# A transformer block in FP32 on TensorE: 32 further tokens of the first expert stage as rows of their own, dot products shared out anew, identity matmuls at the start

## What is computed

```
q = xt @ wq; sub = einsum(q, subkeys)            # scores of 2 x 128 keys, 8 heads
s_top, i_top = top_k(sub, 16)                    # per head and half
cand = s_top[0][:, None] + s_top[1][None, :]
sc, ci = top_k(cand, 16)
eid  = i1 * 128 + i2                             # 128 experts of a token
gate = softmax(sc)
h    = gelu(einsum('cd,ced->ce', x, u[eid]))     # u: 16384 x 1024
out  = einsum('ce,ced->cd', gate * h, v[eid])    # v: 16384 x 1024
h    = layer_norm(ALPHA * h + out)
```

## Time and profile before

| | us |
|---|---|
| median of 3 runs | 1701.08 |
| lowest and highest | 1700.94, 1702.02 |
| profiled execution: its own time | 1701.76 |
| profiled execution: its span | 1700.0 |

### The profile page before, as it was taken

The page is one execution under the profiler, slowest core; times in us unless marked ns, Lnnn a source line. Parts: engine busy times, 40 slices in busy tenths (PEclk is TensorE's granted clock), DMA queues, the critical chain, the costliest instruction groups (busy, mean ns, idle before and its releaser), DMA issues.

```text
span 1700.0 us, 24431 instructions
## 1 busy us (share of the span) xinstructions
PE 1671.8 (98%) x8981; PEld 1477.7 (87%) x8981; DVE 1219.6 (72%) x2490; ACT 778.9 (46%) x1318; POOL 815.4 (48%) x493
## 2 busy tenths in 40 slices
PE   7999999999999999999999999999999999999997
PEld 6777777788889999999999999999888888888886
DVE  3588995512173985989888888434988888888886
ACT  4555544522334444773676477434333333333332
POOL 6232232444551667776866777785523233322312
PEclk9999999999999999999999999999999999999999
DMA  5121122233431566997899789998999999999952
GB/s 203 64 75 50 50 75 75 87 121 116 134 112 38 177 216 197 372 380 253 287 383 371 226 318 374 369 375 291 398 401 349 373 388 349 381 378 353 382 198 87
DMA packets 126502, 417.63 MB, mean 246 GB/s; under 512 B 12976, under 2 KB 32432, under 8 KB 124848
## 3 DMA queue, kind: packets, MB, share of 16 engines
q1 hardware_dynamic: 70320, 232.81, 39.2%
q0 software_dynamic: 36864, 134.23, 21.0%
q10 hardware_dynamic: 19200, 49.03, 7.3%
HBM read 364.91 MB, written 50.86 MB: 245 GB/s over the span
## 4 chain that ended last, share of the span: by engine, by line
PE 92%; DVE 3%; DMA 2%; POOL 1%; ACT 1%; issue 1%; SPq 0%; another core or an unknown queue 0%; ACTq 0%; DVEq 0%; POOLq 0%
PE ps L1364 18%; PE ps L1365 17%; PE ps L1366 17%; PE ps L1602 10%; PE ps L1601 10%; PE ps L1604 10%; PE ps L1712 5%; PE ps L1476 1%; DMA raw<-w_units 1%; PE ps L1428 1%; POOL w_lo L458 1%; PE ps L1459 1%; DMA gelu_d<-gelu_t 1%; PE ps L1405 0%; PE ps L1425 0%
## 5 line engine op out<-in xcount | busy, mean ns | idle before, releaser
L1364 PE MATMUL ps<-tok_hi,w_hi 128*128 128x384 f32 (+1 forms) x1480 | 529.8, 358 | 5.6 <-issue 4.3
L559 ACT ACTIVATE w_hi<-raw 128x1024 fp32r<-128x1024 f32 x330 | 348.9, 1058 | 394.0 <-PE ps L1604 292.3
L1366 PE MATMUL ps<-tok_hi,w_lo 128*128 128x384 f32 (+1 forms) x1480 | 520.5, 352 | 0.0
L1365 PE MATMUL ps<-tok_lo,w_hi 128*128 128x384 f32 (+1 forms) x1480 | 520.5, 352 | 0.0
L502 POOL TENSOR_TENSOR w_lo<-raw,w_hi 128x1024 fp32r<-128x1024 f32 x128 | 318.5, 2491 | 165.6 <-ACT w_hi L559 165.1
L458 POOL TENSOR_TENSOR w_lo<-raw,w_hi 128x1024 fp32r<-128x1024 f32 x76 | 183.3, 2415 | 320.9 <-ACT w_hi L559 320.7
L1364 PEld LDWEIGHTS ps<-tok_hi,w_hi 128*128 128x128 f32 x1480 | 278.2, 188 | 37.2 <-issue 14.5
L519 POOL DMA_INDIRECT v_got<-v_rows,eid x128 | 152.4, 1191 | 301.7 <-DVE own L1148 284.8
L1601 PE MATMUL ps<-w_hi,gh_hi 128*128 128x512 f32 x760 | 295.7, 389 | 0.0
L1602 PE MATMUL ps<-w_lo,gh_hi 128*128 128x512 f32 x760 | 295.7, 389 | 0.0
L1366 PEld LDWEIGHTS ps<-tok_hi,w_lo 128*128 128x128 f32 x1480 | 278.1, 188 | 18.6
(11 more groups left out here) (240 smaller groups left out, 1941.4 us busy)
## 6 DMA issues: line engine op xcount, KB each, us to landing
raw<-u_units SPq DMA_DIRECT2D x128, 512.0 KB
raw<-v_rows SPq DMA_DIRECT2D x128, 512.0 KB
raw<-w_units SPq DMA_DIRECT2D x78, 512.0 KB
gate_d<-stage ACTq DMA_DIRECT2D x12, 2048.0 KB
gelu_d<-gelu_t ACTq DMA_DIRECT2D x120, 192.0 KB
gelu_in<-gelu_d SPq DMA_DIRECT2D x30, 768.0 KB, 7.7
gate_in<-gate_d SPq DMA_DIRECT2D x28, 768.0 KB
gate_in<-gate_d SPq DMA_DIRECT2D x2, 1536.0 KB
```

The costliest lines, as they stand in the source:

```text
L559: act.activation(hi_of(n), raw[:, n % RAW, :], ACT.Copy).then_inc(hi_done, 1)
L1364: pe.matmul(out_, l_hi, r_hi, start=start, stop=False)
L1365: pe.matmul(out_, l_hi, r_lo, start=False, stop=False)
L1366: return pe.matmul(out_, l_lo, r_hi, start=False, stop=stop)
```

## The change

The dense part of the `u` stage takes 352 columns instead of 384. The first 32 tokens of the second tile ("near") get their Gelu values from gathered rows: 32 more gathers and dot products, four groups of 32 columns beside each other, which fill 128 partitions. Their experts are spread over the partitions by four small transfers on ACT's queue (`spread_near_eid`), their `x` rows likewise (`spread_near_x`), and their results go back by four more (`finish_near`). Their gates are still built densely, but last of all quads and already multiplied with the Gelu values; so PE turns picks a fourth time (`turn_picks(4)`), ahead of quad 88, and `gelu_in` holds ones in their columns. The `v` stage keeps its 384 columns.

Around this the table is a new one: 14 first units; 19 units for each route; 13, 17 and 21 units of marks, with 24, 32 and 40 quads; 6 units behind (`TAIL` is 122). The 160 dot products are shared out as 14, 16 and 16 in the routes, at six places of each instead of three; 24, 32 and 38 in the marks; 6 behind; and 14 in the first units of `v`, where the sums with rows of `v` now begin at unit 16 and are due by unit 120 (before: 2 and 116). DVE marks two quads with one pair of instructions. POOL issues gathers in the marks up to `DOTS_BY[k - 2]` plus five. SP issues the first loads of the gates behind the loads of all units of `u`. At the start, PE runs 16 matmuls of the identity with itself (as soon as POOL has made it), and unit 1 runs its products with high weights first.

```diff
-FIRST_UNITS, ROUTE_UNITS, MARK_UNITS = 16, 14, 16
-TAIL = FIRST_UNITS + 3 * (ROUTE_UNITS + MARK_UNITS)
-ROUTE_DOTS, MARK_DOTS = (3, 6, 6), 30
+FIRST_UNITS, ROUTE_UNITS, MARK_UNITS = 14, 19, (13, 17, 21)
+TAIL = FIRST_UNITS + 3 * ROUTE_UNITS + sum(MARK_UNITS)
+ROUTE_DOTS, MARK_DOTS, TAIL_DOTS, LATE_DOTS = (14, 16, 16), (24, 32, 38), 6, 14
+NEAR_FROM, NEAR_END = 58, 58 + NEAR
...
-FMA_START, FMA_END = 2, P - 12
+FMA_START, FMA_END = LATE_DOTS + 2, P - 8
...
             for j in range(P):
                 load_unit(U_EXP + j, u_units[j])
-                if j == P - 8:
-                    sp.wait_ge(gate_read, N_QUAD)
-                    for s in range(2):
-                        sp.wait_ge(stage_out[s], 16 * (NB // 2))
-                    load_gates(0, 0)
-                if j == P - 4:
-                    load_gates(0, 1)
+            sp.wait_ge(gate_read, N_QUAD)
+            for s in range(2):
+                sp.wait_ge(stage_out[s], 16 * (NB // 2))
+            load_gates(0, 0)
             for j in range(P):
                 load_unit(U_VAL + j, v_rows[:, (j - KEPT) % P, :])
+                if j == 1:
+                    load_gates(0, 1)
...
-                rows_to(dots_by(k - 1) + U_SLOTS if k >= FIRST_UNITS + ROUTE_UNITS else 3)
+                if k < FIRST_UNITS + ROUTE_UNITS:
+                    rows_to(min(DOTS_BY[k - 1] + 3, ROUTE_DOTS[0]))
+                else:
+                    rows_to(DOTS_BY[k - 2] + U_SLOTS)
...
+            def finish_near():
+
+                act.wait_ge(dot_done, NEAR_END)
+                act.activation(near_dot[:], near_dot[:], ACT.Gelu).then_inc(near_gelu, 1)
+                act.wait_ge(near_gelu, 1)
+                for g in range(NEAR_GROUPS):
+                    part = slice(NEAR * g, NEAR * g + NEAR)
+                    act.dma_start(near_h[0:NEAR, part], near_dot[part, :]).then_inc(near_h_in, 16)
...
             def mark(q):
...
                 if q >= 4:
-                    dve.wait_ge(gate_full, q - 3)
+                    dve.wait_ge(gate_full, q - 2)
...
-                dve.tensor_tensor(left[:, s, :, :], numbers, first, ALU.is_equal)
-                dve.tensor_tensor(match[:, s, :, :], numbers, second, ALU.is_equal).then_inc(match_set, 1)
+                two = slice(q % 4, q % 4 + 2)
+                dve.tensor_tensor(left[:, two, :, :].rearrange("p s t k -> p (s t) k"), numbers, first, ALU.is_equal)
+                dve.tensor_tensor(match[:, two, :, :].rearrange("p s t k -> p (s t) k"), numbers, second, ALU.is_equal)\
+                    .then_inc(match_set, 1)
...
-                tokens = slice(P, S) if n >= U_EXP else slice(0, S)
-                to = ps[:, bank, 0:DT] if n >= U_EXP else ps[:, bank, :]
+                tokens = slice(P + NEAR, S) if n >= U_EXP else slice(0, S)
+                to = ps[:, bank, 0:UT] if n >= U_EXP else ps[:, bank, :]
...
+            def warm_up():
+
+                pe.wait_ge(const_step, 2)
+                for _ in range(WARM):
+                    pe.matmul(ps[:, 7, 0:P], ident[:], ident[:], start=True, stop=True)
+
+            warm_up()
             first_unit()
+            second_unit()
...
             def turn_picks(b):
-                pe.wait_ge(pick_set, b + 1)
+                if b == NT:
+                    pe.wait_ge(near_pick, 1)
+                    pe.wait_ge(match_set, (N_QUAD - NEAR // 4) // 2)
+                    pe.wait_ge(right_dve, (N_QUAD - NEAR // 4) // 4)
+                    pe.wait_ge(gate_full, N_QUAD - NEAR // 4)
+                else:
+                    pe.wait_ge(pick_set, b + 1)
...
+                    for quad in quads_of(b, k):
+                        if b == NT - 1 and tile_quad(quad) == (NT, 0):
+                            turn_picks(NT)
+                        gates_of(quad)
...
                 for t in range(1, NT):
-                    last = add_tile(n, t, gh_hi[:, j % 4, :], gh_lo[:, j % 4, :], j == 0, False, t - 1)
+                    if j == 0 and t == NT - 1:
+                        pe.wait_ge(bank_read, BANK_EXP + P)
+                    last = add_tile(n, t, ffn_bank(t), gh_hi[:, j % 4, :], gh_lo[:, j % 4, :], j == 0, False, t - 1)
```

303 lines of the change are left out of this document (216 added, 87 removed).

## The result

The changed kernel takes 1741.1 us (median of 6 runs, 1732.0 to 1745.5) against 1701.0 for the kernel before: a ratio of 1.0225, with a 95% interval of 1.0208 to 1.0243. I had written 1690, with a range that ended at 1710. The profiled execution took 1734.84 us, with a span of 1733.1, 33 us more than the one of before.

A forecast was written before the change was run, and what follows sets the result against it. TensorE, busy in 98% of the span, was taken to bound the kernel. 1701.8 - 41.0 - 1.5 + 5 + 14 + 12 = 1690.3, with the median 0.7 lower: 1690 us; range 1662 to 1710.

The forecast's parts named there:

- Columns: Expert matmuls of `u`: 352 instead of 384 columns save 13.3 ns for each of 128 x 24 matmuls, 41.0 us.
- Start: First units: identity matmuls bring the upper clock level earlier, unit 1 no longer waits for low weights; -1.5 us (-2.2 to +0.5).
- Routes: Route stretches: DVE's own work and 14 to 16 dot products, 64 of 73 us, still fit; counted as nothing.
- Fourth turn: Ahead of quad 88: PE's turn, DVE's copy and marks and ACT's scaling are not hidden; +5 us (4 to 6.5).
- Gathers: Marks: gathers issued one unit later take 7.1 us against 5.4 allowed, stalling eight runs by 1.7 us each; +14 us (0 to 38).
- Border: Between `u` and `v`: PE waits for the last gates to be stored and loaded again; +12 us (6 to 22).
- `v` stage: Second half: DVE and DMA take the late dot products and added bytes with little slack; nothing added.
- B: Rival, marks: late gathers delay dot products, marks, scaling and the next gathers; 1722 us, or 1710 in a milder case; chance 0.17.
- C: Rival, marks: bound by bytes, 296 to 310 us where PE wants 281.7; upper end 1704 us, chance 0.09.
- A: Rival, marks and border: gathers land under 5.4 us and the stalls hide; 1665 us (1662 to 1674), chance 0.22.
- the waits behind `right`: Sign, marks: PE waits behind ACT's `right` in eight clusters while DVE waits for `u_got`.
- the distance of 3.84 us: Sign, `u` stage: units without marks must be 3.84 us apart, else the columns step is wrong.

The follow-up runs named there:

- e6_short_lo: Kernel before with 352 columns in the expert matmuls, and POOL's subtraction on 8 columns in place of 1024 in the three routing stretches: 1670.9 us.
- e4_columns_only: Kernel before with 352 columns in place of 384 in the expert matmuls and nothing else changed: 1685.9 us.
- e1_gathers_early: Changed kernel with the gathers in the marks issued one unit earlier, as the kernel before did: 1701.0 us.
- e3: Changed kernel with the first two loads of `v` weights issued ahead of SP's wait for the gates' store: 1741.5 us.

## Why the prediction was wrong, step by step

*Columns, -41.0.* The saving itself is real, even 46.1 at a pitch of 158.3. The step failed in that it was added in full. Alone it gives 15 us, and 30 when DVE does not stand behind POOL in the routing stretches. Most of the rest is the pitch of 166.7 (11.1 us in e6_short_lo), whose cause is open.

*Start, -1.5.* Right in kind; 2.5 measured, just beyond the bound of 2.2.

*Routes, 0.* Wrong. I took "64 of 73 us still fits" from DVE's busy time in one stretch, as if an instruction's duration were its own. It is not: it holds what DVE waits for POOL, 13 us in the `u` stage of the kernel before and 37 in the changed one. e4_columns_only and e6_short_lo show what that is worth: 15 us with the columns alone. In the changed kernel PE waits 5.7 us at two turns, and the lower clock follows one of them.

*Fourth turn, +5.* Right: 3.95 us of wait, and 1.7 us at the lower clock behind it, 5.6 together.

*Gathers, +14.* This is the largest step that failed. The place, the mechanism and the count were right: eight waits of over 1 us behind `right` in the marks. The size was not. By the trace those eight waits are 19.7 us, and the marks lose some 11 us more than those of e1_gathers_early to the lower clock and the seams. Five of the eight waits have a tail. By the medians of e1_gathers_early the later issue costs 40 us.

The term put the lower clock at nothing, and both numbers in it were off. It took a latency of 7.1 us because "the short ones are the rule". In the chain of the changed kernel the eight gathers took 13.4, 8.9, 10.7, 8.0, 6.8, 13.3, 11.6 and 8.5 us, 10.2 in the mean. But PE's waits behind them were 3.3, 3.0, 3.2, 1.6, 1.6, 1.1, 3.3 and 2.6 us: a gather of 13.3 us brought a wait of 1.1, one of 6.8 a wait of 1.6. Latency less wait is 5.1 to 12.2 us, 7.7 in the mean, and not one allowance of 5.4. Put the right latency into my sum, and it says 8 x 4.8 = 38 us of waits where there are 19.7. The two errors work against each other. 25 of the 40 us are there in the kernel before with that one edit. How the other 15 divide between shorter units and what else the change puts into the stretches is not shown.

*Border, +12.* Right: SP loads the gates 10.6 us after the end of unit 122 (I had 10), and PE waits 10.3 us in two parts; with the tail at the lower clock some 14. I had the gates as its only cause, and they are, though the weights behind them in SP's queue seemed to be it until e3.

*`v` stage, 0.* 530.1 us from its first matmul to its last, against 522.4: +8 where I had nothing. 4.4 of it are waits for `gh_lo`; two of them follow loads of Gelu values, the longest of which took 20.2 us. Another 1.6 is the lower clock at its start, and the rest I can't place. It was "little slack", as written, and it was not enough.

*The rivals.* B was the nearest (1722). Its argument, that one late dot product delays marks, scaling and the next gather, is what happened, and its 10.1 us a gather is the mean of the chain. That its number comes so near is in part luck: it has 38 us of waits in the marks where there are 19.7, and nothing for the lower clock, the turns and the `v` stage. C is out as the cause: e1_gathers_early moves 370 GB/s from 676 to 750 us and 380 from 828 to 922 us, with PE busy throughout. The engines' share is 0.99 and 1.00 there, so nothing is left over either. A is out. The row that I gave for engines taking turns between queues shows two stores that ACT issued, one behind the other on one queue, so it says nothing of turns between queues. Of the signs that I had named, the waits behind `right`, the fourth turn, the border's wait and SP's load 10 us after unit 122 came; the distance of 3.84 us came as 3.80 or 4.00, and the `v` stage went over 522.

The waits and their tails had no row in this stage of the kernel before, and I counted what a wait costs beyond itself as nothing, instead of leaving room for it in the range. The row of the 4.07 us wait earlier in the same trace would have told.

## What to carry to other kernels

When the bounding engine is made faster by 8%, price every producer behind it again, with its long latencies beside its usual ones, and add what the clock loses behind a wait: look for a wait anywhere in the trace and read the pitch behind it. Issue prefetches as early as the slots allow; here one unit of lead was worth 25 us in a kernel that seemed to have slack. A duration in a timeline can hold a wait behind another engine; compare the longest and the shortest duration of instructions of one shape before counting on it.
